# Two norm rows before each expert stage: loaded as one partition each and spread over 128 partitions by TensorE and ScalarE

## What is computed

```python
for i in range(DEPTH):                       # DEPTH = 2
    ...                                      # attention, its output is y
    x = layer_norm(DEEPNORM_ALPHA * x + (1 + g1) * y, ln_g[i, 0], ln_b[i, 0])
    h = x * (1 + sc2) + sh2
    y = hierarchical_moe(h, ...)             # 32 experts, 2 per token
    x = layer_norm(DEEPNORM_ALPHA * x + (1 + g2) * y, ln_g[i, 1], ln_b[i, 1])

def layer_norm(x, g, b):                     # over the last axis
    return (x - mu) * rsqrt(var + LN_EPS) * g + b

def expert_block(xb, e):
    return (silu(xb @ w_gate[e]) * (xb @ w_up[e])) @ w_down[e]
```

## Time and profile before

| | |
|---|---|
| three runs | 1516.74, 1512.55, 1517.01 us (median 1516.74) |
| the profiled execution | 1517.6 us, its span 1515.9 us |
| mean granted TensorE clock | 0.958 of full speed |
| TensorE busy | 1375.5 us (91%) |
| VectorE, ScalarE, GpSimd busy | 550.2, 216.2, 83.6 us |
| DMA | 531.20 MB, mean 350 GB/s |
| the expert stage of layer 0 | about 471 to 915 us |
| the expert stage of layer 1 | about 1059 to 1507 us |

### The profile page before, as it was taken

The page is one execution under the profiler, slowest core; times in us unless marked ns, Lnnn a source line. Parts: engine busy times, 40 slices in busy tenths (PEclk is TensorE's granted clock), DMA queues, the critical chain, the costliest instruction groups (busy, mean ns, idle before and its releaser), DMA issues.

```text
span 1515.9 us, 28729 instructions
## 1 busy us (share of the span) xinstructions
PE 1375.5 (91%) x12954; PEld 876.6 (58%) x12954; DVE 550.2 (36%) x1263; ACT 216.2 (14%) x574; POOL 83.6 (6%) x91
## 2 busy tenths in 40 slices
PE   8999999999999999879879799889999797797796
PEld 4886488578886556436445354467665363353453
DVE  3696669665853221111111106584211111111113
ACT  3230123022332000000000002442000000000000
POOL 3100111000003000000000001100200000000000
PEclk9999999999999999889889899999999899898998
DMA  9657955778869999999999998328999999999995
GB/s 347 234 198 258 335 193 197 285 268 305 308 268 395 416 427 425 427 427 427 428 426 426 428 398 325 111 112 337 424 410 425 427 426 427 426 425 428 426 422 219
DMA packets 94742, 531.20 MB, mean 350 GB/s; under 512 B 5248, under 2 KB 7488, under 8 KB 70800
## 3 DMA queue, kind: packets, MB, share of 16 engines
q1 hardware_dynamic: 91456, 519.40, 84.7%
q0 software_dynamic: 3152, 9.86, 1.8%
HBM read 528.19 MB, written 1.05 MB: 349 GB/s over the span
## 4 chain that ended last, share of the span: by engine, by line
PE 61%; DMA 27%; DVE 8%; SPq 1%; ACT 1%; issue 1%; DVEq 0%; ACTq 0%
PE bk L458 23%; DMA ring<-in_moe_w_down 17%; PE bk L965 17%; DMA AR<-in_moe_w_down 9%; PE bk L999 8%; PE bk L1044 4%; DVE mpart L1142 3%; PE bk L531 3%; PE bk L454 2%; PE bk L709 1%; DVE AR L1134 1%; PE bk L724 1%; SPq L2538 1%; ACT AR L2019 1%; PE bk L680 1%
## 5 line engine op out<-in xcount | busy, mean ns | idle before, releaser
L965 PE MATMUL bk<-ring,AR 128*32 128x128 f32 x4480 | 267.3, 409 | 3.4 <-DMA ring<-in_moe_w_up 3.1
L1134 DVE TENSOR_TENSOR AR<-bk,AR 128x128 f32<-128x128 f32 (+2 forms) x106 | 41.3, 389 | 516.2 <-ACT AR L2019 450.7
L965 PEld LDWEIGHTS bk<-ring,AR 128*32 128x32 f32 x4480 | 176.1, 128 | 85.9 <-DMA ring<-in_moe_w_up 5.2
L965 PE MATMUL bk<-AR 128*32 128x128 f32 x3712 | 222.9, 409 | 2.4 <-DMA AR<-in_moe_w_up 2.0
L2019 ACT ACTIVATE AR<-bk 128x512 f32<-128x512 f32 (+4 forms) x182 | 75.1, 435 | 932.0 <-PE bk L965 757.6
L965 PEld LDWEIGHTS bk<-AR 128*32 128x32 f32 x3712 | 145.3, 127 | 72.7 <-DVE X L1134 4.5
L999 PE MATMUL bk<-ring,AR 128*32 128x512 f32 x544 | 139.1, 708 | 42.4 <-DMA ring<-in_moe_w_down 42.4
L458 PE MATMUL bk<-AR,ring 128*128 128x256 f32 (+1 forms) x832 | 170.7, 364 | 1.6 <-DVE diag L1134 1.6
L458 PE MATMUL bk<-ring,AR 128*128 128x256 f32 (+1 forms) x608 | 159.8, 421 | 1.8 <-DVE diag L1134 1.1
L458 PEld LDWEIGHTS bk<-AR,ring 128*128 128x128 f32 x832 | 147.6, 191 | 21.2 <-issue 3.5
L999 PE MATMUL bk<-AR 128*32 128x512 f32 x352 | 131.6, 714 | 27.7 <-DMA AR<-in_moe_w_down 27.7
(11 more groups left out here) (174 smaller groups left out, 980.8 us busy)
## 6 DMA issues: line engine op xcount, KB each, us to landing
ring<-in_moe_w_gate SPq DMA_DIRECT2D x36, 2048.0 KB, 28.8
ring<-in_moe_w_up SPq DMA_DIRECT2D x34, 2048.0 KB, 26.4
AR<-in_moe_w_up SPq DMA_DIRECT2D x30, 2048.0 KB, 29.0
ring<-in_moe_w_down SPq DMA_DIRECT2D x30, 2048.0 KB, 33.9
AR<-in_moe_w_gate SPq DMA_DIRECT2D x28, 2048.0 KB, 26.7
AR<-in_moe_w_down SPq DMA_DIRECT2D x26, 2048.0 KB, 33.9
ring<-in_ada_w SPq DMA_DIRECT2D x24, 2048.0 KB, 11.0
ring<-in_w_in SPq DMA_DIRECT2D x11, 2048.0 KB, 15.2
```

The source lines that it names most:

```text
L965: ins = eng.matmul(o[32 * f:32 * f + 32, 128 * m:128 * m + 128], XG[u][:, c, 32 * j:32 * j + 32], w[:, c, f::4], start=c == 0, stop=c == N ...
L1134: return eng.tensor_tensor(o, a, b, op)
```

## The change

The two DMAs of `norm_before` now read 4 KB into partition 0 alone, each with its own semaphore. In `experts(i)`, quad 0, after gate and up of the third expert (j = 2) and the turn of the second (`hidden(1)`), TensorE does four matmuls with one row of contraction, two for each row, in banks 5 and 6 by turns; the third waits until ScalarE has drained the first, the fourth until the second is drained. ScalarE copies them to `LN_IN` behind its Silu of the third expert. `finish` on GpSimd waits for the four copies where it waited for the two DMAs. The helper `norm_row` of TensorE takes its banks as an argument; the banks of the `LN_OUT` rows stay what they were.

```diff
-            def norm_row(k, w, dst):
+            def norm_row(k, w, dst, to):
                 for h in range(2):
-                    o = begin((3, 5 if w else 4)[h], "row", k, w, h)
+                    o = begin(to[h], "row", k, w, h)
                     pe.wait_ge(sem("ones"), 1)
                     pe.wait_ge(sem(f"row{k}{w}"), 16)
                     end(eng.matmul(o[:, :], ones[0:1, :], dst[0:1, 512 * h:512 * h + 512], ...), "row", k, w, h)
...
                         if j:
                             hidden(j - 1)
+                        if not q and j == 2:
+                            norm_row(2 * i, 0, LN_IN[0], (5, 6))
+                            norm_row(2 * i, 1, LN_IN[1], (5, 6))
...
# ScalarE, in experts(i)
                         s.tell(act(SG[j % 2], bank("gu", i, q, j)[:, 0:128], ACT.Silu), sem("silu"), n + 1)
+                        if not q and j == 2:
+                            norm_row(2 * i, 0, LN_IN[0])
+                            norm_row(2 * i, 1, LN_IN[1])
...
# GpSimd
-            def norm_row(k, n, dst):
-                small(dst, A[("ln_g", "ln_b")[n]][k // 2, k % 2:k % 2 + 1, :].to_broadcast([P, D]), f"row{k}")
...
-                norm_row(2 * i, 1, LN_IN[1])
+                small(LN_IN[1][0:1, :], A["ln_b"][i, 0:1, :], f"row{2 * i}1")
                 g.wait_ge(sem("raw"), 2 * i + 2)
-                norm_row(2 * i, 0, LN_IN[0])
+                small(LN_IN[0][0:1, :], A["ln_g"][i, 0:1, :], f"row{2 * i}0")
...
             def finish(i):
-                g.wait_ge(sem(f"row{2 * i}"), 32)
+                for n in range(2):
+                    for h in range(2):
+                        g.wait_ge(*drained("row", 2 * i, n, h))
```

More of the change, by code:

```diff
@@ L1047, in experts @@
                     if q == NQ - 1:
-                        norm_row(2 * i + 1, 0, LN_OUT[0])
+                        norm_row(2 * i + 1, 0, LN_OUT[0], (3, 4))
                         o = down_rows()
@@ L1054, in experts @@
                         end_sums(sums)
-                        norm_row(2 * i + 1, 1, LN_OUT[1])
+                        norm_row(2 * i + 1, 1, LN_OUT[1], (3, 5))
                     else:
```

## The result

The changed kernel took 1531.08 us in the median of five runs, against 1515.93 us before: ratio 1.0093, 95% interval 1.008 to 1.0107, so slower by 14 to 15 us. A second measurement gave 1529.44 against 1517.20 us: 1.0084, 1.0071 to 1.0097, slower by 12.2 us. The prediction was 1528.6 us with a range of 1521.5 to 1533.

A forecast was written before the change was run, and what follows sets the result against it. TensorE bounds quads 0 and 1, then DMA from SP's restart behind quad 0. Per layer 3.8 row matmuls plus 2.3 clock less 0.15 slack is 5.95; two layers add 11.9 to 1516.74: 1528.6 us, range 1521.5 to 1533.

The forecast's parts named there:

- Quads 0 and 1 are TensorE's, and SP's issue behind quad 0 sets the stage's end: Expert stages: TensorE sets the time in quads 0 and 1, then DMA at 427 GB/s; SP's issue moves each end.
- Bytes are worth nothing: Loads before quad 0: 1.04 MB saved per layer, value 0, at best 2.4 us if the queue did not run dry.
- the queue would run dry earlier: DMA queue ahead of quad 0's end: bytes saved before the restart only make it empty sooner.
- the restart: SP's issue behind quad 0's down product, at 515.02 and 1103.12 us, where the DMA stream starts again.
- 3.8 us of row matmuls per layer: TensorE in quad 0, before the fourth expert: four row matmuls add 3.82 us; the restart slips 3.8 us per layer.
- The clock falls: TensorE at the row matmuls: granted clock falls to half in both layers, for 3.4 to 7 us; chance 0.66.
- The rival in which it stays up: TensorE's clock does not fall: 7.3 us over both layers, 1524.0 us; a fall in one layer or none, chance 0.20.
- What the fall costs: 2.3 us per layer in the sum: TensorE around the row matmuls: low clock loses 2.3 us per layer, bounds 0 and 3.4, far end 5.1.
- a wait on ScalarE in bank 5: Third row matmul: bank 5 free after 1.76 us, matmul due at 1.91, so no wait; otherwise some tenths.
- 11.9 us forecast: Whole kernel: 5.95 us per layer of row matmuls and clock less slack, 11.9 us for two layers.
- The 0.3 us of slack in layer 0: At the issue of 515.02 some DMA engines still worked, which may hide 0.3 us; 0.15 per layer in the sum.
- `finish` costs nothing, being level with its user: GpSimd's finish ends at 509.9 us, ScalarE's gather of quad 1 needs it at 510.0; 1 or 2 us late costs 0.

The follow-up runs named there:

- bank7: The changed kernel with its row matmuls in banks 5 and 7 in place of 5 and 6; 1525.46 us against 1517.20 for the kernel before.
- dense_extra: The kernel before plus four matmuls per layer with 128 rows of contraction, results unread, at the changed kernel's place; 1524.14 us against 1517.20.
- rows_extra: The kernel before plus four matmuls per layer with 1 row of contraction, results unread, at the changed kernel's place; 1525.59 us against 1517.20.
- rows_q3: The kernel before plus four unread one-row matmuls per layer, behind the third expert of the fourth quad; 1516.86 us against 1517.42.
- small_l1_held: The kernel before with layer 1's two norm rows loaded as 4 KB, not spread, and layer 1's finish waiting for VectorE's counts; 1517.10 us against 1516.08.
- spread: The changed kernel with its four row matmuls apart, one behind each product of the second and third expert, banks 5 and 7; 1536.47 us against 1517.42 before.
- spread_late: Row matmuls set apart between second and third expert's products, as changed kernel otherwise, with GpSimd's finish also waiting for VectorE's writes; 1525.93 us against 1516.76 before.
- small_l1: The kernel before with layer 1's two norm rows alone loaded as 4 KB and not spread; 1521.06 us against 1516.76.

## Why the prediction was right

- **Quads 0 and 1 are TensorE's, and SP's issue behind quad 0 sets the stage's end.** Shown: the slips of that issue (changed kernel 11.0, bank7 8.6, dense_extra 3.56 + 3.55 = 7.1, rows_extra 9.8 us) against the medians' growth (12.2, 8.3, 6.9, 8.4), the unchanged 396 us behind it in every profile and layer, and rows_q3, where the same matmuls cost nothing. The slips and the growth agree within 1.4 us.
- **Bytes are worth nothing.** Shown by rows_extra against bank7 and by small_l1_held. That the queue would run dry earlier was right; the hole opens at the experts' start, some 40 us ahead of the restart, and the dip at the restart deepens by TensorE's slip alone.
- **3.8 us of row matmuls per layer.** Right: 3.72 in bank7's layer 0.
- **The clock falls: right.** It fell in both layers of each kernel that has the four row matmuls in a block, and for as long as forecast (3.4 us in layer 0 and 6.8 in layer 1 of the changed kernel). The rival in which it stays up, as TensorE has no idle time, is refuted by bank7: no wait in the block, and a fall.
- **What the fall costs: 2.3 us per layer in the sum, and this term was mis-sized.** It measured 0.2 us in layer 0 and 1.3 in layer 1. The step that failed took every matmul for one that follows the clock, from the down product's rows; gate and up, which stand behind the rows, do not. The profile of before could have warned: gate and up take 3.87 us for 64 matmuls that stream 128 columns, where 64 of the down product, with the same 32 columns of weights but 512 streamed, take 7.0 (507.89 to 514.89). A quarter of the columns for over half of the time: columns do not set the price of gate and up.
- **A wait that was left out: 1.0 us per layer.** The text looked for a wait on ScalarE in bank 5 and took bank 6 for free. The program shows an older result in it, whose drain (VectorE at 497.52 above) stands behind the third expert; in the trace of before it ran from 496.04 to 496.46, 1.9 us behind 494.57, where the second row matmul was due 0.95 behind.
- **Sum.** 11.9 us forecast, from 3.8 + 2.3 - 0.15 per layer; the trace has 3.7 + 1.0 + 0.2 and 3.7 + 1.0 + 1.3. Two errors of opposite sign made a sum that fits the measured 12.2, and 15.2 less well; that it fits so closely is luck. The 0.3 us of slack in layer 0 can't be told: the 396.3 us behind the issue became 395.9, but rows_q3, whose layer 0 is that of before up to there, has 395.9 too. Why the first measurement gave 3 us more than the second stays open; their intervals overlap.
- **`finish` costs nothing, being level with its user.** Right, but by luck. The text asked whether it comes too late. What matters more is what runs beside it: some 2 us earlier it would have run into VectorE's group, as in spread, and nothing in the prediction looked for that.

No version here beats the kernel before.

## What to carry to other kernels

Before counting bytes or idle engines as gain, find the one issue or instruction at which a stage's parts are coupled, and price everything by how far it moves that. A matmul with one row of contraction costs as much as one with 128 (3.72 against 3.53 us for four), may pull the clock down, and needs a bank whose last reader is done. A slow load can be what keeps two engines apart: when it gets fast, look at what starts earlier beside what.

## What the runs showed of the hardware

- Gate and up matmuls (128 rows, 32 columns of weights in each of four column groups, 128 columns streamed) take 3.87 to 3.90 us for 64 at 1.2 GHz and at 2.4 GHz; matmuls with 512 columns in such groups take 1037 against 594 ns, and the gather with 128x128 weights 6.33 against 3.81 us for 32.
- Eight instructions in a row with 1 row of contraction pull the granted clock to half (rows_extra), at the same place where eight with 128 rows leave it at full (dense_extra). Two by two, with 64 gate or up instructions between the pairs, they leave it at full (spread_late).
- A VectorE operation of 0.16 us with both inputs in SBUF took 2.83 us beside a GpSimd product of 2.88 us (small_l1).
